# Attention rounds in mirrored pairs, S5 outputs in double groups, and sample keys loaded apart from values

## What is computed

```python
proj = rmsnorm(x) @ w_in              # u (512) | q (8 heads x 64) | k,v cmp/sel/win (2 kv heads x 64 each) | gates
ssm_out = glu(gelu(s5(u)))            # branch A: complex diagonal state space, then y * sigmoid(y @ w_glu + b)
# branch B, sparse attention: three attentions, mixed by sigmoid gates g
kcmp = gelu(blocks(k_cmp) @ w1) @ w2  # one key per 64 tokens; the same for vcmp; samples: 2048 cached tokens
o = g0 * softmax(q kcmp) vcmp \
  + g1 * softmax(q k_sel[top 16 blocks]) v_sel[top 16 blocks] \
  + g2 * softmax(q k_win) v_win       # window of 512
x = x + rmsnorm((sigmoid(m0) * (ssm_out @ w_br_ssm) + sigmoid(m1) * (o @ w_br_nsa)) @ w_out)
x = x + rmsnorm(cross_attention(rmsnorm(x), memory))
x = x + rmsnorm(relu(rmsnorm(x) @ w_up) ** 2 @ w_down)
```

## Time and profile before

| | us |
|---|---|
| median of 3 runs | 1177.56 (1175.68 to 1180.75) |
| the profiled execution | 1172.68 |
| its span, first to last instruction | 1171.0 |
| mean granted TensorE clock | 0.991 |
| TensorE busy | 1119.5 (96%) |
| VectorE, ScalarE, GpSimd busy | 664.6, 485.7, 168.9 |
| DMA | 164.23 MB, mean 140 GB/s |

### The profile page before, as it was taken

One profiled execution on the slowest core, in us unless ns is written; L12 is line 12 of the kernel. 1 busy time (PEld: TensorE's weight loads), 2 busy tenths in 40 slices (PEclk: granted clock), 3 DMA queues, 4 the chain that ended last, 5 costly groups with the idle time before them and its releaser, 6 DMA issues.

```text
span 1171.0 us, 22135 instructions
## 1 busy us (share of the span) xinstructions
PE 1119.5 (96%) x8538; PEld 1003.8 (86%) x8538; DVE 664.6 (57%) x1159; ACT 485.7 (41%) x768; POOL 168.9 (14%) x281
## 2 busy tenths in 40 slices
PE   6999999999999999899998989999999999999997
PEld 5888777777777777699987978899999989999997
DVE  4557993665775433566645677455442345666663
ACT  3100230346766424353333576453432334645541
POOL 1020023845213222000010030001000000001100
PEclk9999999998999999999999999999999999999999
DMA  6791253744728538467457426742533222232201
GB/s 202 171 255 44 83 186 115 196 115 113 173 61 287 172 115 280 132 208 217 158 130 232 151 93 196 252 145 73 179 121 97 73 94 88 73 107 74 73 1 77
DMA packets 167106, 164.23 MB, mean 140 GB/s; under 512 B 41573, under 2 KB 148034, under 8 KB 166874
## 3 DMA queue, kind: packets, MB, share of 16 engines
q1 hardware_dynamic: 157658, 134.84, 38.0%
q0 software_dynamic: 9344, 27.98, 7.8%
HBM read 154.21 MB, written 12.73 MB: 143 GB/s over the span
## 4 chain that ended last, share of the span: by engine, by line
PE 77%; SPq 7%; DVE 6%; issue 4%; ACT 4%; DMA 1%; POOL 0%; DVEq 0%; ACTq 0%
PE banks L1536 23%; PE banks L1790 15%; PE banks L1025 15%; PE banks L1243 3%; SPq L686 2%; SPq L666 2%; PE banks L1487 2%; PE banks L1490 2%; PE banks L1031 2%; PE banks L1451 1%; DVE rounded L2855 1%; PE banks L1355 1%; SPq L715 1%; PE banks L1467 1%; PE banks L1295 1%
## 5 line engine op out<-in xcount | busy, mean ns | idle before, releaser
L1536 PE MATMUL banks<-rounded 128*128 128x288 f32 (+1 forms) x2304 | 297.0, 289 | 3.1 <-DVE rounded L2982 2.6
L1536 PEld LDWEIGHTS banks<-rounded 128*128 128x128 f32 x2304 | 291.3, 188 | 6.7 <-DVE rounded L2982 3.3
L1025 PE MATMUL banks<-arena 128*128 128x256 f32 (+1 forms) x896 | 210.9, 396 | 2.3 <-issue 1.8
L1025 PEld LDWEIGHTS banks<-arena 128*128 128x128 f32 x896 | 169.9, 191 | 36.8 <-issue 1.9
L1790 PE MATMUL banks<-rounded 128*128 128x272 f32 x1536 | 195.0, 289 | 3.8 <-DVE rounded L3164 3.8
L1790 PEld LDWEIGHTS banks<-rounded 128*128 128x128 f32 x1536 | 194.4, 190 | 4.5 <-issue 3.1
L2855 DVE TENSOR_TENSOR rounded<-arena,rounded 128x2048 fp32r<-128x2048 f32 x63 | 146.1, 2319 | 69.2 <-ACT rounded L2006 69.1
L2006 ACT ACTIVATE rounded<-arena 128x2048 fp32r<-128x2048 f32 x63 | 120.1, 1907 | 21.5 <-PE banks L1451 8.9
L3164 DVE TENSOR_TENSOR rounded<-arena,rounded 128x1088 fp32r<-128x1088 f32 x64 | 82.9, 1304 | 60.1 <-ACT rounded L2283 60.1
L2283 ACT ACTIVATE rounded<-arena 128x1088 fp32r<-128x1088 f32 x64 | 71.1, 1114 | 80.9 <-PE banks L1790 79.7
L2124 ACT ACTIVATE arena<-banks 128x256 f32<-128x256 f32 (+1 forms) x64 | 25.5, 398 | 126.4 <-PE banks L1536 126.4
(11 more groups left out here) (444 smaller groups left out, 1488.6 us busy)
## 6 DMA issues: line engine op xcount, KB each, us to landing
arena<-in_w_up SPq DMA_DIRECT2D x22, 1024.0 KB, 5.4
arena<-in_w_down SPq DMA_DIRECT2D x16, 1024.0 KB, 5.2
arena<-in_w_in SPq DMA_DIRECT2D x13, 1024.0 KB, 9.4
upper<-in_cache_nsa_kv SPq DMA_DIRECT2D x64, 128.0 KB, 2.5
upper<-in_cache_nsa_kv POOLq DMA_DIRECT2D x64, 128.0 KB, 4.4
arena<-in_w_out SPq DMA_DIRECT2D x8, 1024.0 KB, 6.7
arena<-in_cache_mem_kv SPq DMA_DIRECT2D x16, 512.0 KB, 7.8
arena<-in_cache_nsa_kv SPq DMA_DIRECT2D x90, 64.0 KB, 2.3
```

What stands on the lines that cost most here:

```text
L1025: ins = mm(bank(b + h, (NA, NB)[h], rows=M), lhsT(k), rhs[:, k, toks], start=(k == 0), stop=(k == K - 1))
L1536: ins = mm(bank(b, N), w[:, k], a[:, k, toks], start=(k == 0 and z == 0), stop=(k == K - 1 and z == 2))
```

## The change

- S5 outputs run in double groups: the terms of two groups q at once, over 8 PSUM banks (`Y_BANK`), with the transposes and the GLU's first products put between them (`y_terms`, `y_rows_T`, `glu_rows`).
- The sample's query and key transposes come after the prompt's.
- Rounds go in pairs: scores of e, values of e-3, transposes of e-2, 16 compression products, transposes of e-1, values of e-2, scores of e+1. VectorE's and ScalarE's orders and `RELAY_AT` follow. The block scores come in two halves (`BLOCK_ROWS`).
- Load places: position rows (`pe_in`) go from SP to POOL, the first weights' second part and `w2` after more row sets, the value weights before row set 10; zeroing of `w1` goes from POOL to VectorE.
- The last rounds are joined with the block values and with gate 0 in two halves (`gate_part`).
- Sample attention: compressed scores and selection of gg = 1 lie behind gates of gg = 0; two key pieces are transposed in one go; the maximum is taken per piece; probabilities use four banks (`PS_BANKS`); values start after the first copy; output transposes lie inside a gate; for gg = 1 keys (`sel_keys`) are loaded as soon as the scores of gg = 0 have used the slot, and values (`sel_values`) apart, each 64 KB a page.

The core of the diff:

```diff
-        YT_BANK = (4, 5, 0, 1)
+        YT_BANK = (4, 5, 6, 7)
+        Y_BANK = (4, 5, 6, 7, 2, 3, 0, 1)
...
-        KT_BANKS = (0, 1, 4, 5)
+        KT_BANKS = (1, 4, 5, 0)
+        PS_BANKS = (4, 5, 2, 3)
+        CS_BANK = (0, 6)
...
+        BLOCK_ROWS = {11: (0, 1), 19: (2, 3)}
+        SC_AT = 18
...
-                RELAY_AT.setdefault((0, 8 * _u - 5 + _k), []).append(4 * _u + _k)
-                RELAY_AT.setdefault((1, 8 * _u + (0, 0, 1, 2)[_k]), []).append(4 * _u + _k)
+                RELAY_AT.setdefault((0, 8 * _u - 4 + _k), []).append(4 * _u + _k)
+                RELAY_AT.setdefault((1, 8 * _u + _k), []).append(4 * _u + _k)
...
+        def sel_keys(eng, kc, known):
...
+            eng.wait_ge(sem("s_mm"), 20 if kc == 0 else KC_ORDER.index(kc) * 4 + 4)
+            for b in range(4):
+                for i in range(4):
+                    eng.dma_start(kv_pg[:, KV_AT[kc], b, i:i + 1, 0:P],
+                                  A["cache_nsa_kv"][0][bass.ds(known[4 + b, kc * 4 + i], 1), :, 2].rearrange("n p g d -> p n (g d)"))\
+                        .then_inc(sem(f"kv_in_{kc}"), 16)
+
+        def sel_values(eng, kc, known):
+
+            eng.wait_ge(sem("page_values"), kc + 1)
+            eng.wait_ge(sem(f"kv_in_{kc}"), 16 * 16 * 2)
...
+                if n == 5:
                     sp.wait_ge(sem("yT_T"), 8)
                     compress_weights(0, 1)
+                if n == 7:
                     for v, name in enumerate(("w_cmpk2", "w_cmpv2")):
...
-                if j in (10, 12):
+                if j in (9, 12):
                     sp.wait_ge(sem("cmp_done"), 3 + (j == 12))
                     compress_weights(1, int(j == 12))
...
+            for i in range(4):
+                y_terms((0, 1), i)
+            pe.wait_ge(sem("lin_out"), done_unit(("gate", 11)))
+            y_terms((2, 3), 0)
+            y_terms((2, 3), 1)
...
+            y_terms((2, 3), 2)
+            y_rows_T(0)
+            y_rows_T(1)
+            y_terms((2, 3), 3)
+            y_rows_T(2)
+            y_rows_T(3)
+            glu_rows(0, 0)
...
+            pair_scores(0)
+            pair_scores(1)
+            cmp1(0, 0, 16)
+            for e in range(2, NPAIR, 2):
+                u, k = e // 8, e % 8
+                pair_scores(e)
+                if e >= 4:
+                    pair_values(e - 3)
+                if k == 0:
+                    cmp2(u - 1)
+                    cmp1(u, 0, 8)
+                pair_T(e - 2)
+                cmp1(u, 8 * k if k else 8, 8 * k + 16)
+                pair_T(e - 1)
+                if e + 1 in BLOCK_ROWS:
+                    block_scores(e + 1)
+                pair_values(e - 2)
+                pair_scores(e + 1)
...
+                sample_keys_T(gg, 0)
+                sample_keys_T(gg, 1)
+                sample_scores(gg, 0)
+                sample_keys_T(gg, 2)
+                sample_keys_T(gg, 3)
+                sample_scores(gg, 1)
+                sample_scores(gg, 2)
+                sample_keys_T(gg, 4)
+                sample_scores(gg, 3)
...
+            for part, name in enumerate(("w1a_zeroed", "w1b_zeroed")):
+                dve.wait_ge(*((sem("yT_T"), 8) if part else (sem("y_mm"), 8)))
+                own(dve.memset(w1[part][0:64, :, 64:P], 0.0))
+                ins = dve.memset(w1[part][64:P, :, 0:64], 0.0)
...
+            for i in range(NPAIR):
+                if i % 2 == 0:
+                    pair_max(i)
+                    if i % 8 == 0 and i:
+                        cmp_take(i // 8 - 1)
+                if i >= 1:
+                    pair_scale(i - 1)
+                if i % 2 == 0 and i >= 4:
+                    pair_out(i - 3, i - 2)
+                if i % 2:
+                    pair_max(i)
```

More of the change, by code:

```diff
@@ L1204, in _, with y_terms @@
[L1204 to L1207 removed]
+            def y_terms(qs, i):
+                outs = [(q * 4 + i, m, bank(Y_BANK[2 * q + m], P, i * P, rows=YROWS)) for q in qs for m in range(2)]
+                for gp, m, out in outs:
+                    g = 2 * gp + m
+                    mm(out, UT[:, g, 0:YROWS], Tz[:, :, g * C_SSM:(g + 1) * C_SSM], start=True, stop=False)
+                for z in range(2):
+                    for gp, m, out in outs:
+                        ins = mm(out, Z[m * 64:m * 64 + 64, z, gp, 0:YROWS], M2[m * 64:m * 64 + 64, z, gp],
+                                 start=False, stop=(z == 1))
+                        if i == 3 and z == 1:
+                            signal(ins, "y_mm")
@@ new lines, in _ @@
+            for i in range(4):
+                y_terms((0, 1), i)
+            pe.wait_ge(sem("lin_out"), done_unit(("gate", 11)))
+            y_terms((2, 3), 0)
+            y_terms((2, 3), 1)
+            pe.wait_ge(sem("y_out"), 1)
+            pe.wait_ge(*step("hfin_ready"))
+            for z in range(2):
+                pe.transpose(bank(4, P, z * P, rows=GP), hfp[:, z], ident)
+            for z in range(2):
+                ins = pe.transpose(bank(4, P, 256 + z * P), hfs[:, z], ident)
@@ new lines, in _, with gate_part @@
+            for m in range(2, 4):
+                for k in range(4):
+                    glu_rows(m, k)
+            def gate_part(m, k0, k1):
+                u = unit["gate", m]
+                if k0 == 0:
+                    pe.wait_ge(sem("lin_out"), 2 * (u - 1))
+                    pe.wait_ge(sem("p_ready"), 2 * NPAIR)
+                c, b = chunk(("gate", m // 2), KD, 256), 2 * (u % 2)
+                for k in range(k0, k1):
+                    for h, toks in enumerate((HA, HB)):
+                        ins = mm(bank(b + h, (NA, NB)[h]), c[:, k, (m % 2) * P:(m % 2) * P + P], actT[:, k, toks],
+                                 start=(k == 0), stop=(k == KD - 1))
+                if k1 == KD:
+                    signal(ins, "lin_done")
@@ new lines, in pair_T @@
+            def pair_T(j):
+                qt = PAIRS[j][0]
+                if (j + 2) % 8 == 0 and j > 0:
+                    pe.wait_ge(sem("cmp_out"), (j + 2) // 8)
+                pe.wait_ge(sem("p_scaled"), j + 1)
+                if j >= 1:
+                    pe.wait_ge(sem("pT_ready"), j)
+                for g in range(2):
+                    for kt in range(qt + 1):
+                        ins = pe.transpose(bank(4 + g, P, kt * P), p_sb[:, j % 2, g, kt * P:(kt + 1) * P], ident)
+                signal(ins, "p_T")
@@ new lines, in _ @@
+            pair_values(NPAIR - 3)
+            cmp2(CU - 1)
+            pe.wait_ge(sem("hz_ready"), CU)
+            pe.wait_ge(*step("pc_ready"))
+            for q in range(4):
+                ins = pe.transpose(bank(6, P, q * P, rows=64), pc_s[:, q * 64:(q + 1) * 64], ident)
+            signal(ins, "pc_T")
+            pair_T(NPAIR - 2)
+            gate_part(0, 0, 4)
+            pair_T(NPAIR - 1)
+            pair_values(NPAIR - 2)
+            pe.wait_ge(*step("blocks_ready"))
+            block_values(2)
```

546 lines of the change are left out of this document (284 added, 262 removed).

## The result

The changed kernel took 1168.73 us (median of 7 runs, 1162.94 to 1174.69) beside 1177.56 us of the kernel before: ratio 0.9941, 95% interval 0.9912 to 0.9969. That is 9 us less, where 24 were predicted, and just above the upper end of the range (1168). The profiled execution took 1166.26 us, 6.4 less than the profiled one of before.

The account below looks back on a forecast made before the run. TensorE's busy time was taken as the bound, with the SP queue sharing the first half of the rounds. Terms 0.6 + 3.8 + 8.5 + 8.0 + 6.6 - 3.4 = 24.1 us took 1177.6 to 1153.5 us, range 1142 to 1168.

Parts of the forecast that it names:

- up to the first scores: Before the rounds: 0.6 us from moving the sample's query and key transposes, 3.8 from S5 outputs in double groups.
- first half of the rounds: Rounds before the third compression unit: it starts at 300.7 us, TensorE idle 8 us for the SP queue; 4.3 us gained.
- second half: Rounds from the third unit on: fewer shape changes 4.9, waits 1.8 less 1.0, tail 1.0, less 2.5 half clock: 4.2 us.
- sample group 0: Sample attention, first group: waits, half clock and shape changes go, probability transposes use four banks; 8.0 us gained.
- sample group 1: Sample attention, second group: selection behind gates, keys loaded earlier; 6.6 us gained, 64 more load issues covered by 22 us.
- falls at key transposes: Sample attention: paired key transposes stand together in four places; two falls to half clock of 1.7 us cost 3.4.
- rival B: First half of the rounds: the SP queue keeps up, so 8 us idle and 2.5 slow clock go; 1143 us; chance 0.15.
- The fixed parts: TensorE blocks in the rounds: each change of shape costs 0.14 to 0.21 us; mirrored pairs save 0.70 per pair, 11 us.
- the S5 blocks: S5 output stage: each block carries 0.16 us fixed; 32 blocks become 16, gaining 2.6 us.
- Rival C: Rounds: odd rounds come too late, 16 pairs lose 0.5 to 1 us each; 1162 to 1166 us; chance 0.18.
- D: Sample attention: clock falls at every pair of key transposes and stays low into the scores; 1163 us; chance 0.08.
- Zeroing: Start of rounds: VectorE pays 7.2 us, gets back 5.2 on relay copies; first maximum 2 us late, TensorE loses 1.4.

Follow-up runs that it names:

- the undo: Changed kernel with the zero blocks of the compression weights written by POOL again, ahead of the position loads; 1164.9 us, ratio 0.9909 to the kernel before.
- one repair alone: Changed kernel with group-1 window keys loaded on SP ahead of the selected values and S5 weights; 1166.5 us, ratio 0.9902 to the kernel before.
- group 1 in order: Changed kernel with SP's group-1 loads in the order TensorE wants them, window values and keys between selected loads; 1155.1 us, ratio 0.9817 to the kernel before.

## Why the prediction was wrong

Each term as it was predicted and as the two profiled executions give it (gain in us):

| term | predicted | measured |
|---|---|---|
| up to the first scores | 4.4 | 5.5 (234.48 to 228.95) |
| first half of the rounds | 4.3 | -2.2 (75.5 became 77.8) |
| second half | 4.2 | -0.4 (75.6 became 76.1) |
| sample group 0 | 8.0 | 7.8 (45.5 became 37.8) |
| sample group 1 | 6.6 | -4.3 (75.6 became 79.9) |
| falls at key transposes | -3.4 | 0 |
| sum | 24.1 | 6.4 |

**Group 1 is the step that failed most** (10.9 us of the 17.7 that are missing). The prediction wrote "SP is done at 50 and POOL at 60 [...], where the first value is wanted at 82. Covered by 22 us". It compared the 64 additional issues with the first user of what they load, and not with the next thing in the queue: the window keys, wanted 67 us after the block end. SP was done with the values at 69 rather than 50, as it read page numbers again: nothing is issued between 401.1 and 410.0, and of the 26.75 us of the 32 key loads the issues are 17, by the row of the values; another 1.8 us it waited for key rows to land. The cost was a wait of 8.0 us, and half clock behind it: 16 transposes took 3.67 us instead of 1.97 and 8 score products 1.94 instead of 1.06, 2.6 us in sum. With the queue in order the group gained 5.4 us (75.6 to 70.2), near the 6.6; 1.0 of the difference lies in the 16 transposes whose keys land one by one. The term was sound; the price beside it was missed.

**First half of the rounds.** The bound was named rightly (an idle TensorE ended by a relay that waited for a DMA) and rival B was wrong, but the queue was sized too short: from the last S5 output to rows 9 (211.0 to 271.6) it took 60.6 us where the sum had 55.5 plus a wait of 0.4, mostly as nine loads with their reads took 13.2 us instead of 9.9 and two weight loads with their gap 4.4 instead of 2.1. Behind that, rows 9 took 6.3 instead of 5.2 us, and rows 10 and 11 with the numbers between them 18.5 instead of 17.4. The unit started at 306.73, not 300.7. TensorE wanted it at 295.1 rather than 292.8. What the prediction took as given, three times 5 us for page numbers, was the larger price: without those reads the idle time was 0.6 us.

**Second half.** The fixed parts came out of it: between the third unit and the block end, scores have 1.9 us less of busy time, compression 1.8 less beside its slow clock, values 0.3: 4.0, where 4.9 were predicted. Half clock took 1.7 (predicted 2.5). Left out was the second half of the block scores, 1.9 us, which now lies here and no longer in the half that waits for the queue anyway; and waits grew from 1.8 to 2.6 instead of falling to 1.0. The block tail of 1.0 isn't seen.

**Right:** the S5 blocks, group 0 (7.8 us for 8.0; its parts add to 7.9, and none of TensorE's waits is left there), full clock in the paired key transposes, an unchanged rest of the kernel. Rival C appeared only as single waits up to 1.27 us, and D not at all: 32 transposes in a row, three times, at 3.66 to 3.71 us with a granted clock of 1.00. The half clock at the fourth key piece of group 1 stands behind the 8.0 us wait. The Trainium skill (TensorE: Matmul & The Clock Gate, Part 4) has it that transposes don't engage full clock; this trace does not agree.

**Zeroing** was mis-explained while its size was near (1.4 for 1.96). The relay copy in the earlier trace rows takes 2.6 us while POOL writes; I took it for the rule, and VectorE's 5.2 us back as certain. The Trainium skill (SBUF — State Buffer, SBUF: two separate sides) describes an exclusive lock on a port that VectorE and POOL share: for f32 copies such as these, whichever of the two starts first holds it for its whole instruction, and POOL's DMA issues need it too. The runs agree in part. One of the two does stand still for the other: in the kernel before they alternated, in the undo and in the changed kernel POOL lost for all eight copies. But in the undo POOL's write of 9.90 us is recorded from 212.55 on, ahead of VectorE's first copy at 212.83, and lost all the same. That the lock is the cause was not tested by itself.

## What to carry to other kernels

When loads are split or moved, list for their queue every entry behind them with the moment at which each is wanted, less the time from its issue to its landing (some 5 us for the 256 KB loads here); slack at the data that was moved says nothing of the entry that now stands behind it. Reads of indices on an issuing queue are queue time like loads (5 us for nine here), and belong where the queue waits for a slot. And repair waits in the order of time but judge them together: here one repair alone moved its wait whole to the next entry (0.4 us gained, which is within the scatter), where the full reordering gave 10.1.

## What I had not expected of the hardware

POOL's instructions, writes as well as load issues, stretched from 1 to 2 us up to 9.9 while VectorE copied 128 x 1024 floats eight times in a row.

Half clock behind an idle stretch is not a fixed price. After 3.0 us of idleness before the third unit, 16 products took 2.12 us in one version and 3.76 in another with the same code there. Late in the kernel, the same 30 products of one column behind the same 2.34 us of idle time took 3.12 us in one experiment (the undone zeroing) and 5.46 in another (group 1 in order). TensorE over these 10 us, in the same order; the stretch of code is shifted by some 5 us between them, as the second started this stage earlier:

```profile
1140.00:1150.00 10.00, 7.66 (x65) 1.00 0.01 2
```
```profile
1140.00:1150.00 10.00, 7.66 (x41) 0.63 0.01 2
```

From the memory stage to the end, the same code took 663.2 to 669.1 us in 14 profiled executions. Summed in pieces of 5 us, busy time times the missing share of the clock came to 2.7 to 10.1 us, and without it 658.7 to 661.4 are left. So two profiled totals can differ by up to 6 us for reasons outside of the edit, in large part the clock; the start of a later stage, or several timed runs, tell a change of 5 us where one profile's total doesn't.
